# Masked attention of the second stack: score steps of the next-but-one unit put two units ahead, the others one step ahead

## What is computed

```python
o_mb = moba_attention(...)   # own 256-block plus the top earlier ones, bias_moba
o_ns = nsa_attention(...)    # compressed, selected and window branches, gated sum
o_df = diff_attention(...)   # softmax1 - lam * softmax2 over 32-wide halves

def _masked_softmax(logits, mask):
    s = jnp.where(mask, logits, NEG_INF_2)
    m = jnp.max(s, axis=-1, keepdims=True)
    e = jnp.where(mask, jnp.exp(s - m), 0.0)
    return e / jnp.maximum(jnp.sum(e, axis=-1, keepdims=True), TINY)
```

## Time and profile before

| what | us |
|---|---|
| median of 3 runs (lowest, highest) | 2962.5 (2960.69, 2965.73) |
| the profiled execution: device time | 2958.24 |
| its span in the profile | 2956.4 |
| masked attention, layer 0, first matmul to last mix (1665.72 to 1808.71) | 142.99 |
| the same, layer 1 (2393.80 to 2538.98) | 145.18 |
| TensorE busy over the span | 2853.4 (97%) |
| VectorE, ScalarE busy | 1404.8 (48%), 1070.8 (36%) |

### The profile page before, as it was taken

How to read it: one execution, slowest core, us unless ns; L and a number is a source line. 1 busy time by engine, 2 the same in 40 slices (tenths; PEclk the granted TensorE clock), 3 DMA queues, 4 the chain that set the end, 5 groups by cost and what they waited for, 6 DMA issues and landing times. The chain is left out here.

```text
span 2956.4 us, 46483 instructions
## 1 busy us (share of the span) xinstructions
PE 2853.4 (97%) x18586; PEld 2449.9 (83%) x18586; DVE 1404.8 (48%) x2277; ACT 1070.8 (36%) x1496; POOL 220.9 (7%) x206
## 2 busy tenths in 40 slices
PE   8999999999999999999999999999999999999998
PEld 7986899999897789999988656788878755688886
DVE  3743477741574257773242554433424365343342
ACT  3244433322324444332233344432423334342332
POOL 0001300001000120000100022000010002200000
PEclk9989999999998999999999899999999989999999
DMA  3200322222120032222242101222223200122222
GB/s 125 100 29 16 131 91 85 85 97 88 63 100 15 30 136 85 85 82 97 77 140 93 58 1 43 86 100 100 99 86 105 106 31 2 58 86 100 99 89 110
DMA packets 44784, 237.04 MB, mean 80 GB/s; under 512 B 4894, under 2 KB 14750, under 8 KB 21872
## 3 DMA queue, kind: packets, MB, share of 16 engines
q1 hardware_dynamic: 34976, 222.09, 21.5%
q10 hardware_dynamic: 9680, 13.17, 1.3%
HBM read 233.09 MB, written 11.59 MB: 83 GB/s over the span
## 5 line engine op out<-in xcount | busy, mean ns | idle before, releaser
L161 PE MATMUL psum<-u_up_a_hi,w_a_hi 128*128 128x264 f32 x1408 | 376.2, 287 | 5.3 <-DVE u_up_a_lo L1895 5.0
L162 PE MATMUL psum<-u_up_a_lo,w_a_hi 128*128 128x264 f32 x1408 | 373.3, 285 | 0.0
L152 DVE TENSOR_TENSOR w_mlp_b_lo<-ring,w_mlp_b_hi 128x1024 fp32r<-128x1024 f32 x128 | 157.0, 1226 | 330.4 <-ACT w_mlp_b_hi L145 330.4
L164 PE MATMUL psum<-u_up_a_hi,w_a_lo 128*128 128x264 f32 x1408 | 286.1, 284 | 0.0
L152 DVE TENSOR_TENSOR w_a_lo<-ring,w_a_hi 128x1024 fp32r<-128x1024 f32 (+1 forms) x154 | 187.1, 1216 | 206.8 <-ACT w_a_hi L145 204.2
L161 PEld LDWEIGHTS psum<-u_up_a_hi,w_a_hi 128*128 128x128 f32 x1408 | 265.1, 188 | 13.1 <-DVE u_up_a_lo L1895 9.7
L145 ACT ACTIVATE w_a_hi<-ring 128x1024 fp32r<-128x1024 f32 (+1 forms) x154 | 161.4, 1049 | 295.8 <-PE psum L164 294.6
L162 PEld LDWEIGHTS psum<-u_up_a_lo,w_a_hi 128*128 128x128 f32 x1408 | 264.7, 188 | 0.1
L145 ACT ACTIVATE w_mlp_b_hi<-ring 128x1024 fp32r<-128x1024 f32 x128 | 135.7, 1060 | 300.3 <-PE psum L164 299.6
L164 PEld LDWEIGHTS psum<-u_up_a_hi,w_a_lo 128*128 128x128 f32 x1408 | 219.5, 189 | 0.0
L161 PE MATMUL psum<-u_up_b_hi,w_mlp_b_hi 128*128 128x512 f32 x512 | 199.6, 390 | 1.0 <-DVE u_up_b_lo L502 1.0
(11 more groups left out here) (457 smaller groups left out, 6450.4 us busy)
## 6 DMA issues: line engine op xcount, KB each, us to landing
ring<-in_wup SPq DMA_DIRECT2D x44, 1024.0 KB, 4.9
ring<-in_wup_b SPq DMA_DIRECT2D x32, 1024.0 KB, 4.8
ring<-in_wdown_b SPq DMA_DIRECT2D x32, 1024.0 KB, 4.8
ring<-in_win SPq DMA_DIRECT2D x22, 1024.0 KB, 4.9
ring<-in_wdown SPq DMA_DIRECT2D x32, 704.0 KB, 4.1
ring<-in_win_b SPq DMA_DIRECT2D x12, 1024.0 KB, 4.8
near_copies<-near_rows ACTq DMA_DIRECT2D x2, 4608.0 KB
ring<-in_wout SPq DMA_DIRECT2D x8, 1024.0 KB, 5.0
```

The costliest lines, as they stand in the source:

```text
L152: nc.vector.tensor_tensor(W["lo"][:, buf, 0:n], W["tiles"][:, slot, at:at + n], W["hi"][:, buf, 0:n].bitcast(F32), ALU.subtract).then_inc( ...
L161: nc.tensor.matmul(out[c], a_hi, b_hi, start=start, stop=False)
L162: nc.tensor.matmul(out[c], a_hi, b_lo, start=False, stop=False)
L164: mm = nc.tensor.matmul(out[c], a_lo, b_hi, start=False, stop=stop)
```

## The change

In the loop the score steps of a unit move ahead. A unit's steps 0 and 1 stand in the loop pass two units earlier, step 0 between T3 and M2 and step 1 between the turn and M3; steps 2 and 3 take the places that steps 1 and 2 had. `late` names the units for whose successor this does not hold: where the successor is a unit of the selected branch, whose scores need the rows of maxima and the ranks, the old places stay. VectorE's maxima and splits move in the same way. Ahead of the loop stands one more score step, S(1,1), and one more maxima. T3 stands ahead of S(n+1,3) everywhere. The side work moves one unit on where it is 1, 2 or 3 (to units 2, 3 and 4); group 0 stays in unit 1, now behind M1. Where `select` stood behind unit 3's bias, it now stands behind unit 4's, and behind the two maxima of unit 6.

```diff
-    SIDES = (1, 2, 3, 7)
+    SIDES = {1: 0, 2: 1, 3: 2, 4: 3, 7: 7}
+    late = [m + 1 >= U or "selected" in UNITS_B[m + 1] for m in range(U)]
...
-                if (n, step) == (2, 2):
-                    side_read(0)
-                if step == 3 and n - 1 in SIDES:
-                    side_read(n - 1)
+                if step == 0 and n - 2 in SIDES and not late[n - 2]:
+                    side_read(SIDES[n - 2])
+                if step == 3 and n - 1 in SIDES and late[n - 1]:
+                    side_read(SIDES[n - 1])
...
             turn_top(0)
+            score(1, 1)
             for n in range(U):
                 following = n + 1 < U
+                two_on = n + 2 < U and not late[n + 1]
                 transposed(n, 0)
...
-                    score(n + 1, 1)
+                    score(n + 1, 1 if late[n] else 2)
 
                 transposed(n, 1)
                 mix(n, 0)
-                if n == 1:
-                    side(0, K * (n + 1) + 2)
                 if following:
-                    score(n + 1, 2)
+                    score(n + 1, 2 if late[n] else 3)
 
                 transposed(n, 2)
                 mix(n, 1)
                 if n in SIDES:
-                    side(n, K * (n + 1) + 3)
-                    transposed(n, 3)
+                    side(SIDES[n], K * (n + 1) + (3 if late[n] else 4))
+                transposed(n, 3)
+                if following and late[n]:
                     score(n + 1, 3)
-                else:
-                    if following:
-                        score(n + 1, 3)
-                    transposed(n, 3)
+                if two_on:
+                    score(n + 2, 0)
                 mix(n, 2)
 
                 if following:
                     turn_top(n + 1)
-                if n + 2 < U and "selected" not in UNITS_B[n + 2]:
-                    score(n + 2, 0)
+                if two_on:
+                    score(n + 2, 1)
                 mix(n, 3)
-                if n + 2 < U and "selected" in UNITS_B[n + 2]:
+                if n + 2 < U and late[n + 1]:
                     score(n + 2, 0)
...
-                    if (n, step) == (1, 1):
+                    if (n, step) == (1, 2):
...
             maxima(1, 0)
+            maxima(1, 1)
...
                 if following:
-                    maxima(n + 1, 1)
+                    maxima(n + 1, 1 if late[n] else 2)
 
                 add_bias(n, 1)
                 if following:
-                    maxima(n + 1, 2)
+                    maxima(n + 1, 2 if late[n] else 3)
+                    if not late[n]:
+                        split_maxima(n + 1)
 
                 add_bias(n, 2)
-                if n in (1, 2):
-                    mix_compressed(n)
-                if n == 3:
+                if n in (2, 3):
+                    mix_compressed(n - 1)
+                if n == 4:
                     take_importance()
-                if n in SIDES:
-                    add_bias(n, 3)
-                if following:
+                add_bias(n, 3)
+                if following and late[n]:
                     maxima(n + 1, 3)
                     split_maxima(n + 1)
-                if n not in SIDES:
-                    add_bias(n, 3)
                 if n == 0:
                     compressed(2)
-                if n == 3:
-                    select()
...
                 if n + 2 < U:
                     maxima(n + 2, 0)
+                if two_on:
+                    maxima(n + 2, 1)
+                if n == 4:
+                    select()
```

## The result

The changed kernel takes 2981.46 us (median of 7 runs, 2974.04 to 2988.23) against 2962.5 us (7 runs beside it, 2956.72 to 2966.23): a ratio of 1.0064, 95% interval 1.0051 to 1.0077. It is slower by 19 us (15 to 23). The prediction was 2973.4 us, +10.9. The profiled execution took 2983.92 us, its span is 2982.2 us.

What follows compares the result with a forecast made beforehand. It took TensorE, plus short waits in its order, as the bound. Order +2.5 and clock falls +8.4 on 2958.24 gave 2969.1 us for the profiled execution; +10.9 on the median 2962.5 gave 2973.4 us, range 2962 to 2983.

Steps and rivals of the forecast that it cites:

- the clock's part: Falls of the granted clock behind new TensorE gaps: three shorter falls of 2.8 us each, +8.4 us.
- the four gaps: New TensorE idles, two per layer: about 1.6 us behind unit 0's turn, 2 us in unit 5's opening.
- (1): Sign in unit 0: S(2,1) waits 1.3 to 2 us for VectorE's maxima, M3(0) some 2 us later.
- (2): Sign in unit 5's opening: M0(5) waits on ScalarE about 2 us behind the selection, lines 3099 to 3106.
- (3): Sign: granted clock at half behind at least two of the four new gaps.
- (4): Sign in unit 1: the 1.11 us wait before score step (2, 2) gone, unit near 11.9 us.
- (6): Sign: units 7 and 9 stay as before.
- (5): Sign: unit 5 longer by 1.5 to 2 us even at full clock.
- Rival 2: Clock falls behind all four gaps for the longer stretch, slow starts end later: +22.3 us, 2985 us; chance 0.15.
- Rivals 3 and 4: VectorE's blocks hurt less, order denser: 2955 to 2956 with a fall spared, 2959 without; chance 0.06 each.
- V: Experiments' theory: VectorE's softmax and selection blocks, ahead of what TensorE waits for, make the gaps in units 0 and 5.
- Rival 1: Stalls in units 0 and 5 exist but clock holds or falls once: +2.5 to +5.3, 2965 to 2968; chance 0.18.

Runs made afterwards that it cites:

- z3: Changed kernel, order untouched, with idle matmuls in its two new gaps per layer and in the waits of units 7 and 8: 2969.48 us, ratio 1.0036.
- y2: Kernel before, with only idle matmuls added in the waits of units 7 and 8: 2952.48 us, ratio 0.9970.
- x3: Changed kernel with idle matmuls in the two new gaps, in unit 0 and ahead of unit 5's first mix: 2979.56 us, ratio 1.0062.
- z1: Changed kernel with softmax and selection cut up, maxima split late only in units 5 and 6, idle matmuls in units 7 and 8: 2954.77 us, ratio 0.9980.
- x1: Changed kernel with the split of the maxima put back behind the last bias: 2983.63 us, ratio 1.0073.
- x2: Changed kernel, VectorE's order untouched, with GpSimd's multiplications waiting until the split is done: 2985.4 us, ratio 1.0078.
- y4: Changed kernel with VectorE's two blocks, compressed softmax and selection, cut into pieces: 2969.02 us, ratio 1.0029.
- x4: Kernel before with only the side work moved, including group 0 behind M1 and the selection behind unit 4's bias: 2970.54 us, ratio 1.0024.

## Why the prediction was right and wrong

The sign was right, the time lies in the range, and the size was short by 8 us. That the range covers it is owed to the clock's part: what the order costs, +8.1 us, lies outside the -2 to +7 that the prediction gave it. The units of z3 less those of y2 give the changed order's cost nearly free of falls (all but unit 0, which begins in the slow start, run at 1.00):

| Term, per layer | Predicted | Measured |
|---|---|---|
| Unit 0 | +2.3 | +2.5, +2.4 |
| Unit 1 | -2.4 | -2.3, -2.2 |
| Units 2 and 3 | -0.4 | -0.4, -0.3 |
| Unit 4 | +0.7 | +0.5, +0.5 |
| Unit 5 | +1.75 | +2.6, +2.7 |
| Unit 6 | -0.8 | +1.35, +1.35 (the second by the changed kernel's 12.97, since z3 has a fall there) |
| Unit 8 | +0.1 | -0.25 |
| Sum | +1.25 | +3.9, +4.2 |
| Falls behind the four gaps, both layers | +8.4 | +11.2 (changed kernel less x3, by windows; with the difference in the slow start) |

Two layers: 8.1 + 11.2 = 19.3 us, where the medians show 19. That they meet so closely is partly luck. The 11.2 us come from one execution in which all four gaps brought a fall, and neither x3's total nor z3's shows them. What is shown is each part by itself, not that the loss of an average execution is their sum.

Right were, by the prediction's own list: (1) S(2,1) waits 1.73 us for line 3013; (2) M0(5) waits 1.89 and 1.88 us behind lines 3099 to 3106; (3) the clock at half behind these gaps; (4)'s wait gone, unit 1 at 11.81. The stall of unit 0 was worked out by following VectorE's queue from the earlier trace rows. From M1 to M3 it is worth 2.0 us (7.38 against 5.40, z3 and y2), not 2.3. The other 0.5 us of unit 0 stand in its opening, where S(1,2) waits 0.68 us for VectorE's maxima, which the prediction had only as a bound. The estimate for score steps that stand alone in unit 5, +0.6 us from M1 to M3, came out as well: 5.59 us in z1, where nothing waits there, against 5.11 in y2. Of (6) unit 9 held; unit 7 of the first layer took 17.88 us in place of 15.17, by a fall behind an unchanged wait of 1.30 us.

**The step that failed** is the cost of the moved split. The part on unit 6 counts what is gained where the split no longer stands ("T3 no longer waits on VectorE behind the split") and puts nothing for the place where it now stands, in unit 5 as in unit 6. It weighed only VectorE's own queue and did not ask what GpSimd does there. The answer was in the trace of before. In its unit 6 the new place is ahead of the bias of T2, in the middle of GpSimd's train, while the old place lies just behind it:

```profile
1759.25 1.28 POOL L3188 TENSOR_TENSOR y_b<-y_b,at_part_y 128x512 f32<-128x512 f32 x1
1759.69 0.70 DVE L3050 TENSOR_TENSOR psum<-psum,strips 128x512 f32<-128x512 f32 x1
...
1760.48 1.29 POOL L3194 TENSOR_TENSOR fm_lo<-y_b,fm_hi 128x512 fp32r<-128x512 f32 x1
...
1761.80 0.16 DVE L3021 TENSOR_TENSOR top<-top 128x4 f32<-128x4 f32 x1
```

x1 and x2 show it from two sides, 2.3 and 1.2 us in unit 6. With it, unit 5 comes to +1.75 plus the M2 wait of 1.08, and unit 6 to -0.8 plus 2.25, near to what was measured (in unit 6 the order itself was worth -1.2 and -1.0 us, z1 less y2, rather than -0.8). Point (5), unit 5 longer by 1.5 to 2 us even at full clock, was too low for this reason (2.6).

**The term that was mis-sized**, for the profiled execution, is the clock's: three falls at 2.8 us were four, between 1.7 us (behind S(2,1), by the length at half) and 3.5 (unit 5). Three in four was no bad guess all the same. x1 and x2 have seven more such waits, of 1.71 to 2.28 us, and the clock fell behind four of them; with the changed kernel's that makes 8 of 11. Filled (x3, z3) the same gaps brought no fall in 8 of 8. The prediction set beside its own sum that all four gaps would cost, 11.2 us, by what the Trainium skill (TensorE: Matmul & The Clock Gate, A second HAM failure mode: psum-queue depth-cycling) tells of short idles that make the clock swing. The changed kernel's profile agrees with it, the three waits without a fall in x1 and x2 do not.

Not in the sum at all was the stage's start. S(1,1) ahead of T0(0) waits for VectorE's maxima, 0.62 us in z3. Over all thirteen profiles the 18 starts with S(1,1) took 12.9 to 16.6 us, 15.6 on average, the 8 without it 12.4 to 15.6, on average 14.5: about 1 us per layer, within a scatter of 3 us. Rival 2 had the four falls, but at 4.2 us each. Rivals 3 and 4 fell with V: the blocks cost what they were said to, and y4, which cuts them up, gives 10 to 12 us back. Rival 1, the clock holding, fell with the four windows of this execution; x1 and x2 show that it is true of single gaps.

What stays open is why behind an equal wait the clock falls once and not another time: unit 7 of the kernel before (15.17 and 19.33 us, at 1.30 us of wait) shows it, and unit 0 of the first layer with a fall (changed kernel, 1.73 us of wait) and without (x1, 2.28 us; x2, 1.71). No run here tells what decides. Open too is why filling the four new gaps gave back 0.6 to 1.9 us in total and not some 10, and where 6 to 8 us of the distance between z3 and y2 lie. Nor is it shown what the 1.14 us in x4's unit 5 are.

## What to carry to other kernels

Before moving small VectorE operations that read and write SBUF, lay GpSimd's row of the timeline beside their new place: the path that ends last may pass through 0.18 us that become 1.2. When score steps are pulled ahead, every block in front of the maxima they wait for moves onto TensorE's path, so cut the block or pull less. A wait of about 1 us that can't be removed on TensorE can be filled with idle matmuls; here that alone was worth more than any order tried (2952.5 us, ratio 0.997). And a gain or loss found in the windows of one execution has to be looked for in the medians as well: here a part of 11 us didn't show there.

## What the runs showed of the hardware

- A tiny VectorE operation on SBUF operands (128x4 or 128x8) beside a GpSimd `tensor_tensor` of 1.27 to 1.30 us lasts until that one ends: 1.08 to 1.27 us in place of 0.16 to 0.18 when it starts near the other's beginning (changed kernel, units 3 to 6). One that starts just ahead of GpSimd's is not held: line 3036 takes 0.17 us from 1741.21, with line 3191 starting at 1741.22. The bias (line 3050), which reads PSUM, is not held beside the same train: 0.69 us for 512 columns from 1728.82, with GpSimd's line 3191 running from 1728.75 for 1.29 us (changed kernel, unit 3).
- Idle stretches of 0.57 and 1.14 us, with 0.6 us of matmuls between them, were followed by a fall; with them the unit was 7.7 us longer (x4). Waits of 1.7 to 2.3 us were followed by one in 8 of 11 cases (changed kernel 4 of 4, x1 and x2 4 of 7), waits of 1.30 us in unit 7 in 14 of 16, waits of 1.11 us in unit 8 in 15 of 16; a wait of 1.11 us in unit 1 of the kernel before in neither layer.
- Idle matmuls in a wait held the granted clock at 1.00 (units 7 and 8 in 20 of 20 cases, the two new gaps in 8 of 8) and don't delay what the wait ends with: M0(5) starts 3.07 us behind T0(5) in the changed kernel (1751.01 - 1747.94) and in x3 (1752.11 - 1749.04), while unit 7's 19.33 us became 15.19, unit 5's 16.64 became 13.18.
